# GLA's gate path placed between the panels of the in-projection, in a two-layer decoder kernel

## The chip, the cores and the metric

The kernel runs on one core of a Trainium2 chip. The metric is the device time of one execution in microseconds, the median of several runs. The engines are named as in the profile: PE (TensorE's matmuls) and PEld (its weight loads), DVE (VectorE), ACT (ScalarE), POOL (GpSimd) and SP (SyncE, which issues the weights' transfers).

## What is computed

Two decoder layers over 256 tokens of width 1024. Each layer has a mixer, a cross-attention into 256 memory tokens and a feed-forward part (dense in layer 0, top 2 of 8 experts in layer 1). The mixer projects x once and splits the result among differential attention (A), dilated attention (B) and gated linear attention, GLA (C). The change is about GLA's forget gate:

```python
h = x @ w_in
qa, ka, va, qb, kb, vb, qc, kc, vc, gc, rc = jnp.split(h, IN_BOUNDS[1:-1], axis=-1)
...
log_a = jax.nn.log_sigmoid((rc @ gla_wa2 + gla_ba).astype(f32)) / C_GATE_TAU
oc = gla_chunked(qc..., kc..., vc..., log_a...)
```

`rc` has 16 columns (the rank). `log_a` has 4 heads of 48 columns. GLA needs running sums of `log_a` along the tokens and exponentials of their differences; this kernel forms them by levels: for each of 7 block sizes the sums minus their value in the middle of the block, and an eighth plane for what goes from the first 128 tokens to the last 128.

## The kernel before

The program is written out by hand for each engine; instructions run in the order written, and semaphores tie the engines. Nothing is scheduled by a planner.

**In-projection.** Six panels of 512 columns, `gemm(l, n)`, n = 0 to 5. An f32 product is made of three products of a high and a low part (`x_hi`, `x_lo`; the weights' high part is a cast by ACT, `split_high`, L612, the low part a subtraction by DVE, `split_low`, L953). A panel is 48 matmuls of 128x512 on PE (two token tiles of 24, L1559) and goes to PSUM banks 0 and 1 or 2 and 3 in turn. ACT takes token tile 0 to `h` (L578) and DVE tile 1 (L893). The raw weights arrive by SP's queue into five ring slots, each half panel as soon as the half that had its slot is used up; the high parts go to other "homes" by the table `high_homes`.

**The gate path before.** After panel 5 PE computes the rank products (L1624, 24 matmuls, high and low parts of x and `w_rank`; the low part `wr_lo` is DVE's L1031). Then seven rounds of `turn_heads` (L1639, four transposes each) bring the heads of A, B and C with the tokens into the free dimension; ACT (L686, L690) and DVE (L1038) copy them to `tr`. Then come the two matmuls of the gate projection (L1653), and the first scores.

**Attention units.** Seven units u = 0 to 6. The order on PE is: scores of unit u+1 (L1670), part of the memory's key and value projection (`piece`, L1587), the turned probabilities of unit u (L1694), one more piece, the values (L1713). DVE masks the scores and takes their maximum (`masked_max`, L1051 and L1059) for unit u+1, then weighs the two maps of unit u (`difference`, L1071 to L1079), for which PE waits at L1694. ACT does the exponentials (L697). Between these stands the rest of the gate path: the bias and |z| (DVE L1098, L1100) after unit 0's mask, Exp and Ln (ACT L704, L705), the clamp and the sum into `cpad` (DVE L1115 to L1122) in unit 0, an eighth round of `turn_heads` on PE after unit 0's values, ACT's copy of it (L723), the scans (DVE L1128) in unit 1, the level exponents (L1091, L1137, L1139) in units 1 to 3. ACT takes their absolute value (L726) in unit 4 and their exponential (L728) in unit 5. GLA's products by level follow after unit 6. POOL zeroes `qk[:, 1]`, which had held the running sums, when the exponents are done.

## Time and profile before

| what | value |
|---|---|
| median of 3 runs | 1767.54 us (1765.96 to 1773.88) |
| the profiled execution's own time | 1766.63 us |
| its span, first to last instruction | 1764.8 us |
| mean granted TensorE clock | 0.990 |
| PE busy | 1707.9 us, 97% of the span |
| DVE busy | 1331.5 us, 75% |
| ACT busy | 1017.0 us, 58% |
| POOL busy | 22.1 us, 1% |
| chain of waits by engine | PE 88%, DVE 7%, DMA 2%, ACT 2%, issue 1% |

The span is what the sums below are made in; the profiled execution's own time is 1.83 us longer, and 0.91 us under the median. The share of an engine is over all stages: the mixer that the change is in takes the first 185 us of layer 0 and some 175 us of layer 1 (from 470 us), the experts most of the rest.

### The profile page before, as it was taken

What the parts mean: (1) busy time and instruction counts of PE and PEld (TensorE: products, weight loads), DVE (VectorE), ACT (ScalarE), POOL (GpSimd) and SP (SyncE); (2) the same over time, 40 slices, a digit from 0 to 9 for tenths busy, and PEclk for the clock granted to TensorE, in tenths of its full rate; (3) what the DMA queues carried; (4) which work ended last, traced back from release to release, by engine and by line L of the source; (5) the groups of instructions that cost most, each with busy time, mean ns of one, the idle gap of its engine ahead of it and who ended that gap; (6) DMA issues with size and microseconds to landing.
All of it is one profiled execution on the core that took longest, in us unless ns stands there. A gap on an engine that the chain in (4) does not pass through costs nothing.

```text
span 1764.8 us, 21663 instructions
## 1 busy us (share of the span) xinstructions
PE 1707.9 (97%) x7978; PEld 1366.6 (77%) x7978; DVE 1331.5 (75%) x1229; ACT 1017.0 (58%) x895; POOL 22.1 (1%) x32
## 2 busy tenths in 40 slices
PE   7989999999998999899999999999999999999996
PEld 6845787887785577787888888888888888888884
DVE  4566856545655586579799899898898998998996
ACT  4344344434334434267677777777777776776772
POOL 0001000000000100000000000000000000000000
PEclk9999999999999999899999999999999999999997
DMA  8512435546453234589999999999999999999990
GB/s 299 193 53 91 167 120 191 191 143 215 167 193 118 96 127 159 200 295 360 338 366 373 338 367 368 338 356 366 356 362 352 354 367 339 366 369 341 364 373 31
DMA packets 206471, 465.98 MB, mean 264 GB/s; under 512 B 11952, under 2 KB 14544, under 8 KB 206416
## 3 DMA queue, kind: packets, MB, share of 16 engines
q1 hardware_dynamic: 200880, 463.76, 73.7%
q10 hardware_dynamic: 5536, 1.48, 0.4%
q8 instruction: 36, 0.59, 0.1%
q14 instruction: 19, 0.16, 0.0%
HBM read 464.16 MB, written 1.05 MB: 264 GB/s over the span
## 4 chain that ended last, share of the span: by engine, by line
PE 88%; DVE 7%; DMA 2%; ACT 2%; issue 1%; ACTq 0%; DVEq 0%; SPq 0%
PE ps L1559 19%; PE ps L2019 17%; PE ps L2021 17%; PE ps L2020 17%; PE ps L1587 5%; PE ps L1936 3%; PE ps L1996 2%; PE ps L1516 1%; PE ps L2005 1%; DVE w_lo L965 1%; DVE ring_r L953 1%; PE ps L1713 1%; DMA ring<-in_w_in_dram 1%; PE ps L1768 1%; DMA ring<-in_xa_wq_dram 1%
## 5 line engine op out<-in xcount | busy, mean ns | idle before, releaser
L965 DVE TENSOR_TENSOR w_lo<-ring,w_hi 128x2048 fp32r<-128x2048 f32 x336 | 768.1, 2290 | 112.6 <-ACT w_hi L631 109.7
L631 ACT CAST w_hi<-ring 128x2048 fp32r<-128x2048 f32 x336 | 641.8, 1911 | 277.6 <-PE ps L2021 264.1
L2019 PE MATMUL ps<-w_hi,xe_hi 128*128 128x512 f32 x896 | 353.3, 394 | 1.8 <-DVE w_lo L965 1.8
L2021 PE MATMUL ps<-w_hi,xe_lo 128*128 128x512 f32 x896 | 349.4, 390 | 0.0
L2020 PE MATMUL ps<-w_lo,xe_hi 128*128 128x512 f32 x896 | 348.8, 389 | 0.0
L1559 PE MATMUL ps<-ring_r,xT_r 128*128 128x512 f32 (+1 forms) x760 | 199.5, 392 | 1.5 <-ACT ring_r L612 1.1
L2019 PEld LDWEIGHTS ps<-w_hi,xe_hi 128*128 128x128 f32 x896 | 168.3, 188 | 37.2 <-DVE w_lo L965 2.7
L2021 PEld LDWEIGHTS ps<-w_hi,xe_lo 128*128 128x128 f32 x896 | 168.2, 188 | 35.7
L2020 PEld LDWEIGHTS ps<-w_lo,xe_hi 128*128 128x128 f32 x896 | 168.4, 188 | 33.8
L2019 PE MATMUL ps<-w_hi,he_hi 128*128 128x512 f32 x448 | 178.2, 398 | 0.0
L2021 PE MATMUL ps<-w_hi,he_lo 128*128 128x512 f32 x448 | 174.9, 390 | 0.0
L2020 PE MATMUL ps<-w_lo,he_hi 128*128 128x512 f32 x448 | 174.4, 389 | 0.0
L1559 PEld LDWEIGHTS ps<-ring_r,xT_r 128*128 128x128 f32 x760 | 140.6, 189 | 34.4 <-issue 1.5
L1587 PE MATMUL ps<-ring,memT 128*128 128x512 f32 x256 | 120.8, 601 | 0.0
L953 DVE TENSOR_TENSOR ring_r<-ring,late_r 128x2048 fp32r<-128x2048 f32 (+1 forms) x36 | 79.9, 2231 | 32.4 <-ACT late_r L612 31.8
L2021 PEld LDWEIGHTS ps<-w_hi,he_lo 128*128 128x128 f32 x448 | 84.1, 188 | 18.0
L2020 PEld LDWEIGHTS ps<-w_lo,he_hi 128*128 128x128 f32 x448 | 84.3, 188 | 16.2
L2019 PEld LDWEIGHTS ps<-w_hi,he_hi 128*128 128x128 f32 x448 | 84.2, 188 | 16.1
L953 DVE TENSOR_TENSOR ring_r<-ring,ring_r 128x2048 fp32r<-128x2048 f32 (+1 forms) x28 | 63.1, 2252 | 35.6 <-ACT ring_r L612 34.8
L612 ACT CAST late_r<-ring 128x2048 fp32r<-128x2048 f32 (+1 forms) x36 | 66.8, 1862 | 30.3 <-DMA ring<-in_w_in_dram 11.8
L612 ACT CAST ring_r<-ring 128x2048 fp32r<-128x2048 f32 (+1 forms) x28 | 52.7, 1882 | 45.4 <-DMA ring<-in_w_in_dram 24.5
L1587 PEld LDWEIGHTS ps<-ring,memT 128*128 128x128 f32 x256 | 44.4, 190 | 39.7 <-issue 38.7
(266 smaller groups left out, 1803.0 us busy)
## 6 DMA issues: line engine op xcount, KB each, us to landing
ring<-in_moe_w_dram SPq DMA_DIRECT2D x336, 1024.0 KB, 5.8
ring<-in_ffd_w_dram SPq DMA_DIRECT2D x31, 1024.0 KB, 5.2
ring<-in_w_in_dram SPq DMA_DIRECT2D x24, 1024.0 KB, 6.1
ring<-in_xa_wkv_dram SPq DMA_DIRECT2D x16, 1024.0 KB, 5.0
ring<-in_w_out_dram SPq DMA_DIRECT2D x8, 1024.0 KB, 5.1
ring<-in_xa_wq_dram SPq DMA_DIRECT2D x8, 1024.0 KB, 5.2
ring<-in_xa_wo_dram SPq DMA_DIRECT2D x8, 1024.0 KB, 5.2
ring<-in_ffd_w_dram SPq DMA_DIRECT2D x4, 512.0 KB, 3.5
```

Of the source, the lines that this page charges most:

```text
L612: act.copy(high_half(*name), as_high(raw_half(*name), *name)).then_inc(dense_hi, 1)
L631: act.copy(w_hi[:, q % SPLIT_SLOTS, :], ring[:, q % RAW_SLOTS, :]).then_inc(hi_ready, 1)
L953: dve.tensor_tensor(as_high(low_half(*name), *name), as_high(raw_half(*name), *name), high_half(*name).bitcast(F32), ALU.subtract).then_in ...
L965: dve.tensor_tensor(w_lo[:, q % SPLIT_SLOTS, :], ring[:, q % RAW_SLOTS, :], w_hi[:, q % SPLIT_SLOTS, :].bitcast(F32), ALU.subtract).then_i ...
L1516: ins = pe.transpose(ps[:, 4 + b, c * P:(c + 1) * P], src[:, t, k * P:(k + 1) * P], ident)
L1559: ins = pe.matmul(ps[:, b, 0:w], lhs, weights, start=(step == 0), stop=(step == STEPS - 1))
L1587: ins = pe.matmul(ps[:, piece_bank(i), :], memT[:, k, t * P:(t + 1) * P], raw_half(l, IN_P + n, g)[:, c, :], start=(k == 0), stop=(k == KC ...
L1936: ins = pe.matmul(ps[:, t + 2 * col, :], (h_hi, h_lo)[p][:, k, t * P:(t + 1) * P], weights[q][:, c, col * N:(col + 1) * N], start=(k == 0 ...
L1996: ins = pe.matmul(ps[:, 6 + b, c * P:(c + 1) * P], x[:, t, k * P:(k + 1) * P], sel[:, t, :], start=(t == 0), stop=(t == T - 1))
L2019: pe.matmul(ps[:, bank, :], x_hi, hi[:, c, cols], start=first, stop=False)
L2020: pe.matmul(ps[:, bank, :], x_hi, lo[:, c, cols], start=False, stop=False)
L2021: return pe.matmul(ps[:, bank, :], x_lo, hi[:, c, cols], start=False, stop=last)
```

## The change

All in both layers:

- PE: the rank products stand between panels 2 and 3 (in bank 4), the gate projection between panels 3 and 4 (bank 5), the eighth round of transposes between panels 4 and 5 (bank 6). The waits for the bank copies `acc_taken` move to in front of the first scores, and two waits in units 0 and 1 go.
- ACT: the high part of `w_rank` is cast in panel 1's step, the copy of the rank products stands in panel 2's step, Exp and Ln in panel 3's, the copy of the turned decays in panel 4's.
- DVE: `wr_lo` in panel 1's step, bias to `cpad` in panel 3's, behind its two splits, the scans and all exponents in panel 4's. The running sums have a buffer of their own, `decay_sum`.
- POOL zeroes `qk[:, 1]` at the first scores.
- `rankT` lies in another buffer, and the high part of one half panel per layer goes to another home ("keys"), since the exponents' planes are now written during the in-projection.

The same instructions are executed, none added and none taken away; ACT's three table loads of a layer (Exp, Ln, Exp again) move along.

```diff
+            if n < IN_P and 2 * n + g >= 4 and homes[l, n, g] == "dec_late":
+                homes[l, n, g] = "keys"
...
-                "dec_early": late_r[:, 10240:12288]}
+                "dec_early": late_r[:, 10240:12288], "keys": late_r[:, 4096:6144]}
...
-        rankT = spare[0:CR, 14 * P:16 * P]
+        rankT = late[0:CR, 2048:2048 + S]
+        decay_sum = sb("decay_sum", [P, 2, T, P])
...
-                pool.wait_ge(dec_diff, l + 1)
+                pool.wait_ge(scores_ready, UNITS * l + 1)
                 clear(1)
...
-                    if n == 2:
+                    if n == 1:
...
                         act.copy(wr_hi, w_rank[:, l, :, :]).then_inc(wr_high, 1)
+                    if n == 2:
+                        act.wait_ge(rankT_psum, l + 1)
+                        act.copy(rankT, ps[0:CR, 4, 0:S]).then_inc(rankT_sb, 1)
                         act.wait_ge(lam_dots, l + 1)
                         act.activation(lams[:, 0:2], lams[:, 0:2], ACT.Exp).then_inc(lam_exps, 1)
+                    if n == 3:
+                        act.wait_ge(z_abs, l + 1)
+                        done(act.activation(zz[:, 1, :], zz[:, 1, :], ACT.Exp, scale=-1.0))
+                        act.activation(zz[:, 1, :], zz[:, 1, :], ACT.Ln, bias=1.0).then_inc(z_ln, 1)
                     if n == 4:
+                        act.wait_ge(decT_psum, l + 1)
+                        act.copy(tr[:, 14:16, :], ps[:, 6, :].rearrange("p (b s) -> p b s", b=2)).then_inc(decT_sb, 1)
...
-                act.wait_ge(rankT_psum, l + 1)
-                act.copy(rankT, ps[0:CR, 0, 0:S]).then_inc(rankT_sb, 1)
...
-
-                act.wait_ge(z_abs, l + 1)
-                done(act.activation(zz[:, 1, :], zz[:, 1, :], ACT.Exp, scale=-1.0))
-                act.activation(zz[:, 1, :], zz[:, 1, :], ACT.Ln, bias=1.0).then_inc(z_ln, 1)
...
-                    if u == 0:
-                        act.wait_ge(decT_psum, l + 1)
-                        act.copy(tr[:, 14:16, :], ps[:, 3, :].rearrange("p (b s) -> p b s", b=2)).then_inc(decT_sb, 1)
...
+            def level_exponents(v):
+                half = (P // 2) >> v
+                sums_v = decay_sum[:, :, :, :].rearrange("p a t s -> p (a t s)").rearrange("p (n w) -> p n w", w=2 * half)
+                dve.tensor_tensor(dec[:, v, :].rearrange("p (n w) -> p n w", w=2 * half), sums_v,
+                                  sums_v[:, :, half - 1:half].to_broadcast([P, 2 * S // (2 * half), 2 * half]),
+                                  ALU.subtract)
...
-                    if n == 4:
+                    if n == 1:
                         dve.wait_ge(wr_high, l + 1)
                         dve.tensor_tensor(wr_lo, w_rank[:, l, :, :], wr_hi.bitcast(F32), ALU.subtract).then_inc(wr_ready, 1)
+                    if n == 3:
+                        dve.wait_ge(z_psum, l + 1)
+                        z3 = zz.rearrange("p a (t n) -> p a t n", t=T)
+                        done(dve.tensor_tensor(z3[:, 0], ps[:, 5, 0:T * CH * CK].rearrange("p (t n) -> p t n", t=T),
+                                               ba[:, l, :].unsqueeze(1).to_broadcast([P, T, CH * CK]), ALU.add))
+                        done(dve.scalar_tensor_tensor(zz[:, 1, :], zz[:, 0, :], -1.0, zz[:, 0, :], ALU.mult, ALU.max))
+                        dve.sem_inc(z_abs, 1)
+                        done(dve.tensor_scalar(zz[:, 0, :], zz[:, 0, :], 0.0, 1.0 / TAU, ALU.min, ALU.mult))
                         dve.wait_ge(lam_exps, l + 1)
                         done(dve.tensor_tensor(lams[:, 2:3], lams[:, 1:2], lams[:, 0:1], ALU.subtract))
                         done(dve.tensor_scalar(lams[:, 3:4], lams[:, 2:3], -lam_init, None, ALU.add))
+                        dve.wait_ge(z_ln, l + 1)
+                        done(dve.tensor_scalar(zz[:, 2, :], zz[:, 1, :], -1.0 / TAU, None, ALU.mult))
+                        if l == 0:
+                            dve.wait_ge(pstep, 2)
+                        zh = zz.rearrange("p a (t h k) -> p a t h k", t=T, h=CH)
+                        for t in range(T):
+                            ins = dve.tensor_tensor(cpad[:, t, 2 * CH:3 * CH, 0:CK], zh[:, 0, t], zh[:, 2, t], ALU.add)
+                        ins.then_inc(decay_ready, 1)
+                    if n == 4:
+                        dve.wait_ge(decT_sb, l + 1)
+                        for pair in range(2):
+                            for t in range(T):
+                                ins = dve.tensor_tensor_scan(decay_sum[:, pair, t, :], ones, tr[:, 14 + pair, t * P:(t + 1) * P],
+                                                             0.0, ALU.mult, ALU.add)
+                        done(ins)
+                        for v in range(LEVELS):
+                            level_exponents(v)
+                        d7 = dec[:, 7, :].rearrange("p (a t s) -> p a t s", a=2, t=T)
+                        dve.tensor_tensor(d7[:, :, 0, :], decay_sum[:, :, 0, :],
+                                          decay_sum[:, :, 0, P - 1:P].to_broadcast([P, 2, P]), ALU.subtract)
+                        done(dve.tensor_copy(d7[:, :, 1, :], decay_sum[:, :, 1, :]))
+                        dve.sem_inc(dec_diff, 1)
...
-                for n in range(2, IN_P):
-                    gemm(l, n)
+                gemm(l, 2)
...
-                pe.wait_ge(acc_taken[0], acc_use(l, 4) // 2 + 1)
                 pe.wait_ge(wr_ready, l + 1)
                 for m, (p, q) in enumerate(HI_LO):
                     for k in range(KC):
-                        ins = pe.matmul(ps[0:CR, 0, 0:S], (wr_hi, wr_lo)[q][:, k, :], (x_hi, x_lo)[p][:, k, :],
+                        ins = pe.matmul(ps[0:CR, 4, 0:S], (wr_hi, wr_lo)[q][:, k, :], (x_hi, x_lo)[p][:, k, :],
                                         start=(m == 0 and k == 0), stop=(m == 2 and k == KC - 1))
                 ins.then_inc(rankT_psum, 1)
+                gemm(l, 3)
+                pe.wait_ge(rankT_sb, l + 1)
+                for t in range(T):
+                    ins = pe.matmul(ps[:, 5, t * CH * CK:(t + 1) * CH * CK], rankT[:, t * P:(t + 1) * P], wa2[:, l, :],
+                                    start=True, stop=True)
+                ins.then_inc(z_psum, 1)
...
+                gemm(l, 4)
+                pe.wait_ge(decay_ready, l + 1)
+                turn_heads(7, 6).then_inc(decT_psum, 1)
+                gemm(l, 5)
                 pe.wait_ge(rope_done, l + 1)
+                pe.wait_ge(decT_sb, l + 1)
...
-                pe.wait_ge(acc_taken[2], acc_use(l, 5) // 2 + 1)
-                pe.wait_ge(rankT_sb, l + 1)
-                for t in range(T):
-                    ins = pe.matmul(ps[:, 2, t * CH * CK:(t + 1) * CH * CK], rankT[:, t * P:(t + 1) * P], wa2[:, l, :],
-                                    start=True, stop=True)
-                ins.then_inc(z_psum, 1)
+                pe.wait_ge(acc_taken[0], acc_use(l, 4) // 2 + 1)
+                for b in (2, 3):
+                    pe.wait_ge(acc_taken[b], acc_use(l, 5) // 2 + 1)
                 for b in range(4):
                     pe.wait_ge(tr_sb[b], (2 if b < 3 else 1) * (l + 1))
...
-                    if u == 0:
-                        pe.wait_ge(z_abs, l + 1)
-                    if u == 1:
-                        pe.wait_ge(decT_sb, l + 1)
...
-                    if u == 0:
-                        pe.wait_ge(decay_ready, l + 1)
-                        pe.wait_ge(acc_taken[3], acc_use(l, 5) // 2 + 1)
-                        turn_heads(7, 3).then_inc(decT_psum, 1)
```

The order on PE in layer 0, from the end of panel 2 on, before (a row is an instruction or a run of equal ones with what it waits for; L1559 are panels, L1624 rank products, L1639 `turn_heads`, L1653 the gate projection, L1670 scores, L1713 values; rows between are left out):

```order
L1559 MATMUL ps<-ring_r,xT_r 128x512 x4
L1624 MATMUL ps<-xT_r,wr_split 16x256 [waits const_in,tp_taken3,acc_taken0,tp_taken2,wr_ready,tp_taken1,tp_taken0]
L1624 MATMUL ps<-xT_r,wr_split 16x256 x7
L1639 MATMUL ps<-square,h 128x128 [waits rope_done]
L1639 MATMUL ps<-square,cpad 128x128 [waits tr_sb2]
L1653 MATMUL ps<-wa,ring 128x192 [waits rankT_sb,acc_taken2]
L1670 MATMUL ps<-late 128x128 [waits tr_sb2,tr_sb3,tr_sb1,tr_sb0]
L1713 MATMUL ps<-h,qk 128x64 [waits turn_taken]
L1639 MATMUL ps<-square,cpad 128x128 [waits acc_taken3,decay_ready]
L1670 MATMUL ps<-late 128x128 [waits score_taken]
```

and in the changed kernel (the line numbers are its own: L1557 panels, L1620 rank products, L1626 gate projection, L1641 `turn_heads`, L1674 scores):

```order
L1557 MATMUL ps<-ring_r,xT_r 128x512 x4
L1620 MATMUL ps<-xT_r,wr_split 16x256 [waits tp_taken3,const_in,tp_taken2,wr_ready,tp_taken1,tp_taken0]
L1557 MATMUL ps<-late_r,xT_r 128x512 [waits dense_hi,acc_taken2]
L1557 MATMUL ps<-ring_r,xT_r 128x512 x4
L1626 MATMUL ps<-wa,late 128x192 [waits rankT_sb]
L1557 MATMUL ps<-ring_r,xT_r 128x512 [waits dense_hi,acc_taken0]
L1557 MATMUL ps<-ring_r,xT_r 128x512 x4
L1641 MATMUL ps<-square,cpad 128x128 [waits decay_ready]
L1557 MATMUL ps<-ring_r,xT_r 128x512 [waits dense_hi,acc_taken2]
L1641 MATMUL ps<-square,cpad 128x128 [waits tr_sb2]
L1674 MATMUL ps<-late 128x128 [waits tr_sb1,tr_sb0,tr_sb2,acc_taken3,tr_sb3,acc_taken2,acc_taken0]
```

The rank products, the gate projection and the eighth round moved from behind panel 5 (the last of them from behind unit 0's values) to the three joints between panels 2, 3, 4 and 5.

The order on DVE in layer 0 from the end of panel 1's step to the first masks, before (L893 takes a panel's tile, L1031 is `wr_lo`, L1051 a mask, L1098 and L1100 the bias and |z|):

```order
L1022 TENSOR_SCALAR g_a<-g_a 128x64 [waits vstep]
L893 COPY h<-ps 128x512 [waits acc_ready1,vstep]
L893 COPY h<-ps 128x512 [waits acc_ready1]
L1031 TENSOR_TENSOR wr_split<-w_rank,wr_split 128x128 [waits h_dve,wr_high]
L1033 TENSOR_TENSOR lams<-lams 128x1 [waits lam_exps]
L1051 SCALAR_TENSOR_TENSOR late<-ps,mask_a 128x128 [waits scores_ready]
L1098 TENSOR_TENSOR late<-ps,ba 128x384 [waits vstep,z_psum]
L1100 SCALAR_TENSOR_TENSOR late<-late 128x384 [waits vstep]
L1051 SCALAR_TENSOR_TENSOR late<-ps,mask_a 128x256 [waits vstep,scores_ready]
```

and in the changed kernel (L896 takes a tile, L1041 is `wr_lo`, L956 a split, L1045 to L1059 bias to `cpad`, L1065 the scans, L1010 and L1071 exponents):

```order
L1032 TENSOR_SCALAR g_a<-g_a 128x64 [waits vstep]
L1041 TENSOR_TENSOR wr_split<-w_rank,wr_split 128x128 [waits wr_high,vstep]
L896 COPY h<-ps 128x512 [waits acc_ready1]
L956 TENSOR_TENSOR ring_r<-ring,late_r 128x2048 [waits dense_hi]
L1045 TENSOR_TENSOR late<-ps,ba 128x384 [waits z_psum]
L1049 TENSOR_SCALAR late<-late 128x384 [waits vstep]
L1054 TENSOR_SCALAR late<-late 128x384 [waits z_ln,vstep]
L1059 TENSOR_TENSOR cpad<-late 128x4x48 [waits pstep,vstep]
L896 COPY h<-ps 128x512 [waits acc_ready1]
L1065 SCALAR_TENSOR_TENSOR decay_sum<-square,late 128x128 [waits h_dve,decT_sb]
L1010 TENSOR_TENSOR late<-decay_sum 128x512 x6
```

`wr_lo` now stands ahead of the take of panel 2's tile, the decay's instructions behind the last split of panel 5 and ahead of the take of panel 4's tile, the scans and exponents behind that take.

## Rows read from the trace of the kernel before

**Rows 1.** windows: PE, PEld, DVE, ACT, POOL busy, PEclk, DMA, GB/s:
```profile
90.00:149.00 59.00, 53.20 (x243) 28.47 (x244) 36.38 (x93) 32.30 (x78) 2.60 (x2) 1.00 0.21 72
740.00:750.00 10.00, 5.82 (x26) 5.25 (x24) 7.35 (x20) 0.79 (x2) 0.00 (x0) 0.50 1.04 389
```

**Rows 2.** PE's waits, whole span: us in total, times, longest:
```profile
PE ps L1694 <- DVE late L1079: 10.4, 6, 1.9
...
PE ps L1516 <- DVEq L922: 5.7, 5, 3.4
```

**Rows 3.** timeline of PE, units 0 and 1 of layer 0:
```profile
99.51 0.44 PE L1694 MATMUL ps<-square,late 128*128 128x128 f32 x2 [1.89 <-DVE late L1079]
...
101.03 0.61 PE L1639 MATMUL ps<-square,cpad 128*128 128x128 f32 x4
101.57 0.50 PE L1670 MATMUL ps<-late 32*128 32x128 f32 x8
...
106.07 0.66 PE L1694 MATMUL ps<-square,late 128*128 128x128 f32 x4 [1.22 <-DVE late L1079]
```

**Rows 4.** timeline of DVE, layer 0: masks of units 1, 2, 5:
```profile
94.91 1.42 DVE L1051 SCALAR_TENSOR_TENSOR late<-ps,mask_a 128x256 f32<-128x256 f32 x4 [1.26 <-PE ps L1670]
...
102.14 0.89 DVE L1051 SCALAR_TENSOR_TENSOR late<-ps,mask_a 128x128 f32<-128x128 f32 x4 [1.36 <-PE ps L1670]
...
124.31 1.15 DVE L1051 SCALAR_TENSOR_TENSOR late<-ps,mask_b 128x128 f32<-128x128 f32 x4 [0.47 <-PE ps L1670]
```

**Rows 5.** timeline, PE, layer 0: start, us, line, names, count [idle before <- releaser]:
```profile
49.75 1.09 PE L1559 MATMUL ps<-late_r,xT_r 128*128 128x512 f32 x4
...
83.23 1.08 PE L1624 MATMUL ps<-xT_r,wr_split 128*16 128x256 f32 x8
...
85.97 2.35 PE L1639 MATMUL ps<-square,h 128*128 128x128 f32 x20
...
89.12 0.91 PE L1653 MATMUL ps<-wa,ring 16*128 16x192 f32 x4
90.07 0.50 PE L1670 MATMUL ps<-late 32*128 32x128 f32 x8
```

**Rows 6.** timeline of DVE, layer 0: g_a, panel 5's last split, wr_lo:
```profile
49.51 0.20 DVE L1022 TENSOR_SCALAR g_a<-g_a 128x64 f32<-128x64 f32 x1
...
65.34 2.29 DVE L953 TENSOR_TENSOR ring_r<-ring,late_r 128x2048 fp32r<-128x2048 f32 x1 [1.12 <-ACT late_r L612]
...
73.11 0.29 DVE L1031 TENSOR_TENSOR wr_split<-w_rank,wr_split 128x128 fp32r<-128x128 f32 x1
```

**Rows 7.** timeline of ACT, layer 0: round 6's copy:
```profile
89.23 0.58 ACT L690 COPY late<-ps 128x512 f32<-128x512 f32 x1 [0.29 <-PE ps L1639]
```

**Rows 8.** timeline of ACT, layer 0: panel 5's last cast:
```profile
63.40 1.91 ACT L612 CAST late_r<-ring 128x2048 fp32r<-128x2048 f32 x1 [4.94 <-DMA ring<-in_w_in_dram]
```

**Rows 9.** timeline of DVE, layer 0: the decay's small instructions:
```profile
92.50 0.56 DVE L1098 TENSOR_TENSOR late<-ps,ba 128x384 f32<-128x384 f32 x1
93.09 0.56 DVE L1100 SCALAR_TENSOR_TENSOR late<-late 128x384 f32<-128x384 f32 x1
...
99.76 0.36 DVE L1117 TENSOR_SCALAR late<-late 128x384 f32<-128x384 f32 x1
100.15 0.63 DVE L1122 TENSOR_TENSOR cpad<-late 128x192 f32<-128x192 f32 x2
```

**Rows 10.** timeline of ACT, layer 0: table load and Ln of the decay:
```profile
94.52 1.28 ACT L705 ACT_TABLE_LOAD   x1
95.82 0.52 ACT L705 ACTIVATE late<-late 128x384 f32<-128x384 f32 x1
```

**Rows 11.** groups by line, DVE: the level exponents, both layers: busy us, mean ns:
```profile
L1091 DVE TENSOR_TENSOR late<-qk 128x512 f32<-128x512 f32 x14 | 8.9, 687 | 0.1
```

**Rows 12.** timeline of DVE, layer 1: g_a, last split of panel 5:
```profile
505.40 0.20 DVE L1022 TENSOR_SCALAR g_a<-g_a 128x64 f32<-128x64 f32 x1
...
523.27 2.29 DVE L953 TENSOR_TENSOR ring_r<-ring,ring_r 128x2048 fp32r<-128x2048 f32 x1 [0.92 <-ACT ring_r L612]
```

39 lines of the change are left out of this document (removed).

## The prediction

> **What bounds the kernel.** Four views, in this order. First the windows over the mixer's attention units of layer 0: PE is busy for 53 of 59 us, DVE for 36 and ACT for 32, and PE's granted clock is 1.00, the 2.4 GHz level [rows 1]. Nothing that the change frees on DVE or ACT has a value of its own there; it can pay only where PE waits for it. So second, PE's waits: six waits for `difference` (L1079) add up to 10.4 us over both layers [rows 2], and these are what a lighter DVE could at best shorten. Third, PE in units 0 and 1: it stops for 1.89 us and for 1.22 us ahead of the turned probabilities [rows 3]. Fourth, and this decides, what DVE did ahead of each of these waits. `difference(u)` stands behind `masked_max(u+1)`, and that mask was itself waiting for PE's scores: the mask of unit 1 began after 1.26 us of idle time, that of unit 2 after 1.36 us, and even that of unit 5, which stands behind the last exponents, after 0.47 us [rows 4]. The reader is to see a loop: PE gives scores, DVE masks and weighs, PE waits. The gate path's instructions sit in DVE's idle part of that loop, not in it. Taking them out makes the idle part longer and leaves 1.89 and 1.22 us where they were.
>
> The in-projection, where the work goes, is bound by PE: from the start of panel 3 to the first rank product its matmuls stand without a gap, 33.48 us for three panels, 11.16 us each [rows 5]. Whatever PE gets there is added in full.
>
> **The change part by part.**
>
> *Rank products.* They take 2.74 us (83.23 to 85.97 [rows 5]) and move from behind panel 5 to behind panel 2, both on PE's path: nothing gained. They covered nothing behind panel 5, since the transposes that followed need no part of panel 5. But at the new place they need `wr_lo`, now behind `g_a` on DVE. In layer 0 `g_a` ends at 49.71; with 0.04 us between the two and 0.29 us for the subtraction [rows 6] `wr_lo` is there at 50.04, and PE sees it some 0.06 us later. PE is free at 49.75 [rows 5]: a wait of 0.35 us. In layer 1 `g_a` is done at 505.60 [rows 12], over 2 us before panel 3's old start; no wait. Sum so far +0.35 us.
>
> *Gate projection.* 0.91 us per layer [rows 5] goes between panels 3 and 4, and costs its whole length there. At the old place it was nearly free: it ran from 89.12 while ACT copied the last round of heads, which was in SBUF at 89.81 [rows 7], and the first scores, which need that copy, began at 90.07 [rows 5]. Without it they can begin at about 89.87, so that 0.20 us comes back of 0.91. Net +0.71 us per layer. The bounds are 0 (the copy is not waited for at all) and 0.95 (nothing comes back); I take 0.71, since the copy's row is measured.
>
> *The eighth round.* Behind unit 0's values it kept PE from the scores of unit 2 for 0.54 us (101.03 to 101.57 [rows 3]), on the loop. Seven rounds take 3.15 us (85.97 to 89.12 [rows 5]), so one round between the panels costs 0.45 us. Net -0.09 us per layer.
>
> *The added wait.* The eighth round now stands between panels 4 and 5 and waits for `decay_ready`, and panel 5 is queued behind it, with everything after. The chain to it: DVE's last split of panel 5 follows ACT's cast, and the cast waited 4.94 us for its weights [rows 8], whose slot is freed by panel 3's matmuls. So the chain moves with panel 3, by 2.74 + 0.35 = 3.09 us: the split ends at 65.34 + 2.29 + 3.09 = 70.72 [rows 6]. Then come bias and |z| 0.56 + 0.56, clamp 0.36 hidden beside ACT, Exp about as long as Ln 0.52, table load 1.28, Ln 0.52, the scaling 0.36 and the sums 0.63 [rows 9, 10]: 4.43 us, with six handovers of some 0.05 us 4.7, ready at 75.4. PE is through panel 4 at 49.75 + 2 x 11.16 + 3.09 + 0.91 = 76.07. Slack 0.65 us, no wait. Layer 1 repeats the pattern 457.9 us later (523.27 against 65.34 [rows 6, 12]), without the 0.35 on either side of the comparison.
>
> The table load is where the Trainium skill speaks against the change. In the trace the load takes 1.28 us and Ln starts 0.02 us behind it [rows 10]. ScalarE: Activation LUTs, in "What ACT_TABLE_LOAD costs", gives the same load and adds a drain of about 1.38 us to every switch. By that the chain would end at 76.8, PE would wait 0.7 us in each layer, and the sum would be 3.0 instead of 1.6. No such drain stands in the row, so the sum goes without.
>
> *Scans and exponents.* Seven exponents of 0.687 us [rows 11] and six instructions of half their width or less, which 13 x 0.69 = 9 us bounds from above. They have DVE's idle time beside panel 5's 11.16 us, and the exponentials that need them come in units 4 and 5. ACT's reload of the Exp table falls between its last copy and the first mask's maximum. The wait of POOL for `dec_diff` goes, and the zeroes it writes are needed only by GLA's products, tens of microseconds later. The new home saves a cast a wait on DMA-paced panels. All zero; if the exponents ran late, DVE's take of panel 5 and then the first scores would be late with them.
>
> **Sum.** 0.35 + 2 x (0.71 - 0.09) = +1.6 us, on a span of 1764.8: 1766.4, and 1768.2 with the 1.83 us that lie outside. The median shown is 0.91 above the profiled execution, so against it the forecast is 1767.54 + 1.6 = **1769.1 us**, no change that a measurement of this kernel can tell (about 0.5%, 8.8 us).
>
> **Rivals.**
>
> *A, the waits go.* If the small instructions on DVE did hold back `difference`, the six waits could vanish: 10.4 us less [rows 2], 1767.5 - 10.4 + 1.6 = 1758.7. For it: the work does leave those units. Against it: DVE stood idle for PE ahead of the masks [rows 4]. Half of it would give 1764. Chance 0.04.
>
> *B, the chain to the eighth round is late by a little.* The slack is 0.65 us, and the weights at its head need only arrive later than in this one trace, or the table switch cost more. For it: every link is on another engine and the margin is less than one of them. Against it: all links are measured. From 0.7 to 2 us per layer: 1770.5 to 1773. Chance 0.12. (The case of the skill's drain, 1770.5, lies here, and the trace as it stands gives it a third of that.)
>
> *C, slower: the chain is so late that the clock falls.* PE has been seen to wait for 3.4 us ahead of transposes [rows 2], and in the stretch that holds that place its granted clock was 0.50, the 1.2 GHz level [rows 1]. If PE stood still before the eighth round for as long, say because ACT reaches Exp only behind a late cast, it would lose 3.4 us, and 10 us of panel 5 at half the clock cost 5 more. Twice that is 17 us: 1786. It decides from a chain some 4 us later than reckoned. Nothing in the rows makes it so. Chance 0.03.
>
> *D, the clock's stretch between the layers' end and the experts comes out otherwise.* PE was busy for 5.82 us at half the clock in one 10 us window [rows 1]; at full clock that would be 2.9 us less. A shift of what precedes it could give that back, or take as much: 1766 to 1772. Chance 0.08, split evenly.
>
> **How the numbers follow.** The forecast as it stands has 0.73. It, B and D make the range: from 1769.1 - 2.9 and the 1.6 us by which the lowest of the runs lies under the median, 1764.6, to B's end at 1773: 1764.5 to 1773.5. A's full size and C are outside. Faster by over 0.5% is most of A, 0.03; slower is C, 0.03; the rest, 0.94, is no change.
>
> **What would show it.** In the profile of the changed kernel: PE's wait at the turned probabilities still 1.9, 1.2 to 1.6 and 1.9 us in units 0 to 2; DVE idle for over 2 us ahead of the masks; a wait of about 0.35 us ahead of layer 0's first rank product and none in layer 1; no wait ahead of the eighth round; the gate projection 0.9 us between panels; the first scores of layer 0 about 1.5 us later than before (0.35 + 0.91 + 0.45 - 0.20), and unit 2's scores some 0.5 us less late than that. A median under 1764, or PE's waits for L1079's counterpart well under 10 us in all, would prove the reading of DVE's idle time wrong; a wait of over 1 us at the eighth round would prove the chain's arithmetic wrong.

## The result, and the profile after

The changed kernel takes 1773.78 us (median of 6 runs, 1771.98 to 1775.49), the kernel before in the same comparison 1767.53 us (6 runs, 1765.96 to 1773.88). The ratio is 1.0026, with a 95% interval from 1.0016 to 1.0037: slower by a quarter of a per cent, within the 0.5% that counted as no change here, but a difference that the comparison does resolve. (Of all executions used in this document one, of the kernel before, took 5838 us; it counts in no ratio and no mean below.) The profiled execution took 1771.98 us with a span of 1770.2 us, against 1764.8 us before: 5.4 us more, where 1.6 were forecast. PE is busy for 1711.3 us, and it has 88% of the chain of waits, as before.

PE's waits over the whole span of the changed kernel (us in total, times, longest us):

```profile
PE ps L1694 <- DVE late L1119: 10.4, 6, 2.2
...
PE ps L1674 <- ACT late L700: 1.9, 2, 1.0
```

The first row answers to the first of [rows 2]: the six waits for `difference` (now L1119) come to 10.4 us, to the tenth what they were. Two rows are new: 1.9 us at the first scores (L1674), where PE waits for ACT's copy of the last round of heads, and, not shown here, 0.2 us at the first rank product.

The timeline of PE in layer 0 of the changed kernel (start, us, line, names, count, idle before and releaser), which answers to [rows 3, 5]:

```profile
49.98 1.09 PE L1620 MATMUL ps<-xT_r,wr_split 128*16 128x256 f32 x8 [0.16 <-DVE wr_split L1041]
...
63.97 0.91 PE L1626 MATMUL ps<-wa,late 16*128 16x192 f32 x4
...
76.11 0.60 PE L1641 MATMUL ps<-square,cpad 128*128 128x128 f32 x4
...
89.89 1.04 PE L1641 MATMUL ps<-square,cpad 128*128 128x128 f32 x8
91.80 0.50 PE L1674 MATMUL ps<-late 32*128 32x128 f32 x8 [0.87 <-ACT late L700]
...
101.24 0.44 PE L1694 MATMUL ps<-square,late 128*128 128x128 f32 x2 [1.89 <-DVE late L1119]
...
102.86 0.50 PE L1674 MATMUL ps<-late 32*128 32x128 f32 x8
...
107.36 0.66 PE L1694 MATMUL ps<-square,late 128*128 128x128 f32 x4 [1.22 <-DVE late L1119]
```

The eighth round at 76.11 has no wait. The waits of units 0 and 1 are 1.89 and 1.22 us, as before. The first scores begin 1.73 us later than in [rows 5] (91.80 against 90.07), the scores of unit 2 then 1.29 us later (102.86 against 101.57), since the round that stood ahead of them is gone.

Layer 1 does the same. Its panels begin 3.89 us later than before (the rows at 494.04 and 490.15 further down), and its first scores and unit 1's turned probabilities are these, in the changed kernel:

```profile
553.65 0.50 PE L1674 MATMUL ps<-late 32*128 32x128 f32 x8 [0.98 <-ACT late L700]
...
569.55 0.66 PE L1694 MATMUL ps<-square,late 128*128 128x128 f32 x4 [1.22 <-DVE late L1119]
```

and in the kernel before:

```profile
548.17 0.50 PE L1670 MATMUL ps<-late 32*128 32x128 f32 x8
...
564.53 0.66 PE L1694 MATMUL ps<-square,late 128*128 128x128 f32 x4 [1.57 <-DVE late L1079]
```

Against the layer's start the first scores are 1.59 us later, and by unit 1's turned probabilities 1.13 us are left. So the moved instructions cost 1.29 + 1.13 = 2.4 us in all.

The timeline of DVE in layer 0 of the changed kernel, the same columns:

```profile
49.54 0.29 DVE L1041 TENSOR_TENSOR wr_split<-w_rank,wr_split 128x128 fp32r<-128x128 f32 x1
...
74.50 0.63 DVE L1059 TENSOR_TENSOR cpad<-late 128x192 f32<-128x192 f32 x2
...
96.65 1.42 DVE L1091 SCALAR_TENSOR_TENSOR late<-ps,mask_a 128x256 f32<-128x256 f32 x4 [2.56 <-PE ps L1674]
...
103.43 0.88 DVE L1091 SCALAR_TENSOR_TENSOR late<-ps,mask_a 128x128 f32<-128x128 f32 x4 [2.25 <-PE ps L1674]
```

`decay_ready` comes at 74.50 + 0.63 = 75.13, 0.98 us ahead of PE. The masks of units 1 and 2 now follow 2.56 and 2.25 us of idle time, where [rows 4] had 1.26 and 1.36. The gate path did leave DVE's units 0 to 3, and it turned into idle time there.

The timeline of ACT in layer 0 of the changed kernel, the same columns:

```profile
72.19 1.28 ACT L681 ACT_TABLE_LOAD   x1
73.48 0.53 ACT L681 ACTIVATE late<-late 128x384 f32<-128x384 f32 x1
...
90.97 0.58 ACT L700 COPY late<-ps 128x512 f32<-128x512 f32 x1 [0.29 <-PE ps L1641]
```

Ln starts 0.01 us behind its table load, as in [rows 10]. The copy that the first scores need ends at 91.55, 0.25 us ahead of them. What lies between is in the view of the scores' waits (L1661, from 91.5 us on; PEldq is PE's sequencer; the three numbers are the shortest, median and longest in ns):

```profile
L1661 PEldq EVENT_SEMAPHORE  x2: 51/51/51, 91.6 to 91.7; - x2
```

PE goes through two wait instructions here, at 91.59 and 91.69, before it loads the scores' weights.

**Where the other 3 us come from.** 2.4 us of structure leave 3.0 of the 5.4. Following PE's matmuls of both profiles side by side shows two places where the distance jumps. Windows of the changed kernel there (width, PE, PEld, DVE, ACT, POOL busy, PEclk, DMA share, GB/s):

```profile
410.00:415.00 5.00, 5.00 (x20) 3.98 (x20) 3.83 (x2) 3.64 (x4) 0.00 (x0) 0.76 0.30 120
488.00:491.00 3.00, 3.00 (x7) 2.36 (x8) 0.00 (x0) 0.78 (x1) 0.00 (x0) 0.51 0.00 0
```

and of the kernel before, in the same windows:

```profile
410.00:415.00 5.00, 5.00 (x25) 4.07 (x24) 4.85 (x5) 2.56 (x3) 0.00 (x0) 1.00 0.24 39
488.00:491.00 3.00, 3.00 (x14) 2.40 (x14) 0.00 (x0) 0.00 (x0) 0.00 (x0) 1.00 0.41 98
```

PE is busy throughout in all four, at a granted clock of 0.76 and 0.51 after the change and of 1.00 before: in the latter window it gets 7 matmuls done instead of 14. PE's timeline of the changed kernel around both places:

```profile
408.44 0.70 PE L1931 MATMUL ps<-ring_r,h_r 128*128 128x512 f32 x2 [2.78 <-DVEq L1325]
...
412.85 0.60 PE L1904 MATMUL ps<-square,late 128*128 128x128 f32 x4
...
487.92 2.04 PE L1557 MATMUL ps<-qk_r,xT_r 128*128 128x512 f32 x4 [1.61 <-DVE late_r L947]
...
494.04 1.09 PE L1557 MATMUL ps<-ring_r,xT_r 128*128 128x512 f32 x4
```

and of the kernel before:

```profile
407.39 0.70 PE L1936 MATMUL ps<-ring_r,h_r 128*128 128x512 f32 x2 [2.67 <-ACT ring_r L612]
...
410.25 0.60 PE L1909 MATMUL ps<-square,late 128*128 128x128 f32 x4
...
485.42 1.18 PE L1559 MATMUL ps<-qk_r,xT_r 128*128 128x512 f32 x4 [1.61 <-DVE late_r L944]
...
490.15 1.10 PE L1559 MATMUL ps<-ring_r,xT_r 128*128 128x512 f32 x4
```

Matched in pairs, the distance goes from 1.05 to 2.60 us at the first place (1.55 us) and from 2.50 to 3.89 at the second (1.39 us). The waits ahead of them are nearly the same in both kernels, 2.78 against 2.67 and 1.61 twice. The work and the waits are alike; only the clock granted after the wait differs. That is 2.9 us, and 2.4 + 2.9 = 5.3. The rest of the way isn't flat, but cancels: the distance goes back from 1.29 us at unit 2 to 1.05 at 407 us, by another 0.10 to the second place, and grows by some 0.3 behind layer 1's units.

### The profile page after: what moved, and what is told of

It is laid out like the page before. It is cut to its first block, busy times and chain, and to the rows that moved or that the text cites. A ratio compares the mean times of both kernels' runs of the same rounds, so it can differ in the third digit from the quotient of the medians.

```text
span 1770.2 us, 21661 instructions
## 1 busy us (share of the span) xinstructions
PE 1711.3 (97%) x7978; PEld 1368.9 (77%) x7978; DVE 1331.7 (75%) x1229; ACT 1016.8 (57%) x895; POOL 22.1 (1%) x32
## 3 DMA queue, kind: packets, MB, share of 16 engines
HBM read 464.16 MB, written 1.05 MB: 263 GB/s over the span
## 4 chain that ended last, share of the span: by engine, by line
PE 88%; DVE 7%; DMA 2%; ACT 2%; issue 1%; ACTq 0%; DVEq 0%; SPq 0%
PE ps L1557 19%; PE ps L2014 17%; PE ps L2016 17%; PE ps L2015 17%; PE ps L1585 5%; PE ps L1931 3%; PE ps L1991 2%; PE ps L2000 1%; DMA ring<-in_w_in_dram 1%; PE ps L1514 1%; DVE w_lo L968 1%; DVE ring_r L956 1%; PE ps L1713 1%; PE ps L1763 1%; PE ps L1831 1%
## 5 line engine op out<-in xcount | busy, mean ns | idle before, releaser
L1557 PE MATMUL ps<-ring_r,xT_r 128*128 128x512 f32 (+1 forms) x760 | 200.1, 392 | 1.5 <-ACT ring_r L615 1.1
L1557 PEld LDWEIGHTS ps<-ring_r,xT_r 128*128 128x128 f32 x760 | 140.3, 189 | 34.4 <-issue 1.7
L956 DVE TENSOR_TENSOR ring_r<-ring,late_r 128x2048 fp32r<-128x2048 f32 (+1 forms) x36 | 79.9, 2231 | 33.5 <-ACT late_r L615 33.0
L956 DVE TENSOR_TENSOR ring_r<-ring,ring_r 128x2048 fp32r<-128x2048 f32 (+1 forms) x28 | 63.0, 2251 | 35.8 <-ACT ring_r L615 35.1
```

What stands on the lines that cost most here:

```text
L956: dve.tensor_tensor(as_high(low_half(*name), *name), as_high(raw_half(*name), *name), high_half(*name).bitcast(F32), ALU.subtract).then_in ...
L1557: ins = pe.matmul(ps[:, b, 0:w], lhs, weights, start=(step == 0), stop=(step == STEPS - 1))
```

## The experiments

The two questions were whether the stops at 408 and 488 us belong to the change, and which part of the loop of scores, masks and turned probabilities holds PE for its 1.9 us. All runs stood beside fresh runs of the kernel before on the same chip.

**Lateness alone.** The kernel before, with eight more matmuls ahead of layer 0's rank products (their result is overwritten):

```diff
+                for k in range(8 if l == 0 else 0):
+                    pe.matmul(ps[0:CR, 0, 0:S], wr_hi[:, k % KC, :], x_hi[:, k % KC, :], start=True, stop=True)
```

> The kernel before with 8 more rank matmuls in layer 0 alone (0.91 us on PE, result unused), nothing else. Theory (clock): what follows the mixer of layer 0 is merely late by 0.91 us, about as much as in the changed kernel (0.94 us at 404 us), and that lateness is enough for the granted clock to fall in the wait between the first and the second half of layer 0's feed-forward part: PE loses about 1.6 us there, and the time is 0.9 + 1.6 = 2.5 us above before, or 3.8 us with a second fall at the start of layer 1. Rival (something in the change itself, a buffer or a queue, makes that stretch slower): no fall, +0.9 us.

Measured: 1770.45 us (10 runs), ratio 1.0006 [0.9996, 1.0017], span 1769.8. PE is 0.9 us late from there on. At 408 us the clock stays at 1.00; at 486 us it falls, in a kernel that has nothing of the change. Windows of this kernel (columns as above):

```profile
485.00:488.00 3.00, 1.39 (x9) 1.09 (x7) 1.29 (x2) 2.73 (x3) 0.00 (x0) 0.76 0.00 0
488.00:491.00 3.00, 3.00 (x9) 2.32 (x8) 0.00 (x0) 0.14 (x1) 0.00 (x0) 0.50 0.00 0
```

So the fall at 486 needs nothing of the change. The theory that a later arrival brings the fall at 408 was not borne out by this one profile, and the ratio amounts to 1.1 us, nearer to the rival's 0.9 than to the theory's 2.5. The fall lasts longer than those above, through four windows of 2 us, and costs more: the distance to the kernel before grows from 1.86 to 4.63 us, 2.8 us.

**Rank products alone.** The kernel before with only the rank products, `wr_lo` and the copy of `rankT` moved ahead, and `rankT` at another place of `late`:

```diff
-                for n in range(2, IN_P):
-                    gemm(l, n)
+                gemm(l, 2)
...
-                pe.wait_ge(acc_taken[0], acc_use(l, 4) // 2 + 1)
                 pe.wait_ge(wr_ready, l + 1)
...
                 ins.then_inc(rankT_psum, 1)
+                for n in range(3, IN_P):
+                    gemm(l, n)
+                pe.wait_ge(acc_taken[0], acc_use(l, 4) // 2 + 1)
```

> The rank products alone between panels 2 and 3, with wr_hi and wr_lo in panel 1's step; the gate projection, the eighth round and all of DVE's and ACT's decay work where they were before. Theory: the rank products cost the same in both places, so the first scores of layer 0 start within 0.2 us of before (the 0.16 us wait for wr_lo), those of layer 1 too, and the time is that of before plus 0.2 us, unless the clock falls. Rival (any work put between panels disturbs them): first scores later by 0.5 us or more per layer.

Measured: 1769.9 us (10 runs), ratio 1.0004 [0.9994, 1.0014]. PE's timeline of this kernel, layer 0:

```profile
50.54 1.07 PE L1624 MATMUL ps<-xT_r,wr_split 128*16 128x256 f32 x8 [0.51 <-DVE wr_split L1032]
...
88.93 1.04 PE L1642 MATMUL ps<-square,cpad 128*128 128x128 f32 x8
89.89 0.91 PE L1656 MATMUL ps<-wa,late 16*128 16x192 f32 x4
90.84 0.50 PE L1673 MATMUL ps<-late 32*128 32x128 f32 x8
```

With its wait of 0.51 us for `wr_lo`, PE reaches the rank products 0.79 us after the place that it had for panel 3 in [rows 5], and the first scores begin 0.77 us later than before: moving the rank products costs that delay and nothing else. The 0.2 us expected were too few, and the rival's 0.5 is reached without its reason: no panel is disturbed, PE waits for `wr_lo`. That the wait is 0.16 us in the full change and 0.51 here shows how loosely this term is fixed: it is the place of one short instruction on DVE.

**Filling the new wait.** The changed kernel, with two of the four parts of the mixer's first projection piece put ahead of the first scores:

```diff
+                piece(l, 0, range(0, 2))
                 pe.wait_ge(acc_taken[0], acc_use(l, 4) // 2 + 1)
...
                 scores(0)
-                piece(l, 0, range(0, 4))
+                piece(l, 0, range(2, 4))
```

> The changed kernel, with two of the four chunks of the memory projection that stand behind the first scores put ahead of them (PE's order alone). Theory: the 0.9 us that PE now waits ahead of the first scores for ACT's last copy is filled, 0.87 us less per layer, so that the profile shows no wait there, and the time is 1.7 us below the changed kernel's, 1772. Rival (the first scores are themselves the start of the chain that bounds units 0 to 2, so that any delay of them comes back as a wait): the same time as the changed kernel, with the wait at the turned probabilities of unit 0 longer.

Measured: 1772.55 us (10 runs, the lowest 1770.10, 1.9 below the change's lowest), ratio 1.0017 [1.0007, 1.0027], span 1768.3. PE's timeline of this kernel:

```profile
91.70 1.88 PE L1585 MATMUL ps<-ring,memT 128*128 128x512 f32 x4
93.51 0.50 PE L1675 MATMUL ps<-late 32*128 32x128 f32 x8
...
101.24 0.44 PE L1695 MATMUL ps<-square,late 128*128 128x128 f32 x2 [1.89 <-DVE late L1119]
```

The last round of heads, ahead of the edit, starts here:

```profile
90.82 1.04 PE L1641 MATMUL ps<-square,cpad 128*128 128x128 f32 x8
```

The 0.87 us at the first scores are gone, and the wait of unit 0 is 1.89 us as before. Its turned probabilities start at 101.24, the same number as in the change without the fill, but this execution was 0.93 us late already at the last round of heads (90.82 against 89.89). Counted from that round they come after 10.42 us, where the change takes 11.35: 0.93 us are won. In layer 1 it is 10.77 against 11.81 us (549.03 to 559.80, and 551.63 to 563.44), 1.04 won. So the rows bear out the theory's 1.7 us and not the rival: `difference(0)` stands behind the mask of unit 1, whose scores come 0.93 us earlier, since PE gets to them through the same work without the wait. The first scores come 0.78 us later against the same round, but the wait doesn't depend on them.

The median doesn't show this (1772.55 against 1773.78 and, further down, 1772.65 for the change). By the table of the mean clock below it does: the runs with the fill are shorter by 0.7 to 2.3 us than those of the change at the same mean clock (0.987 to 0.989, nine runs), but their own mean clock is lower (0.9875 over the 10 runs, 0.9884 over the change's 17).

**No scans, no exponents.** The kernel before without `tensor_tensor_scan` and the level exponents; POOL writes zeroes in their place. It leaves out GLA's decays, so only the time up to the end of layer 0's mixer is read.

```diff
+                pool.wait_ge(decay_ready, l + 1)
+                pool.memset(dec, 0.0).then_inc(dec_diff, 1)
...
-                    if 1 <= u < 4:
-                        for v in (range(0, 2), range(2, 4), range(4, LEVELS))[u - 1]:
-                            level_exponents(v)
```

> The kernel before without DVE's scans and level exponents in units 1 to 3 (about 6 us of DVE per layer; POOL writes zeroes in their place, so the decays are left out of the result, and the experts' routing may come out otherwise; only the trace up to the end of layer 0's mixer is compared). Theory: DVE's idle time ahead of the masks of units 2 to 5 grows, and PE's waits at the turned probabilities stay at 1.9, 1.2 and 1.9 us in units 0 to 2. Rival (lighter DVE shortens the waits): they shrink or vanish, and the products of GLA's levels start 1 to 5 us earlier.

Measured: one run, 1776.66 us, span 1774.9. PE's three waits are 1.90, 1.95 and 1.97 us, none shorter than in [rows 3], with DVE idle for 3.27 and 3.59 us ahead of the masks of units 3 and 4. Taking the exponents out of the units gives PE nothing. The 1.95 of unit 1 was a surprise. DVE's timeline of this kernel, and POOL's:

```profile
104.73 1.35 DVE L1077 TENSOR_SCALAR late<-late,rsum 128x256 f32<-128x256 f32 x2
...
104.73 0.95 POOL L539 MEMSET qk<- 128x1024 f32 x1
```

The two instructions take 1.35 us, where the same pair takes 0.62 in the kernel before: POOL's 0.95 us of zeroes for `qk`, which follow the early zeroes in my edit, fell on them, and `difference` was late by the 0.73. The Trainium skill (SBUF — State Buffer, "Who interferes with whom") says that `tensor_scalar` can run in a mode that takes the SBUF ports it shares with GpSimd, and that whichever of the two comes second then blocks fully; the 0.73 us lost beside 0.95 us of memset agree with it. It is one occurrence, and no run was made for it.

**The change once more**, unaltered.

> The changed kernel again, unaltered, beside the others on one chip, for more executions and a second profile. Theory: each execution has a few short falls of the granted clock behind PE's waits, one to four of them, in places that differ from one execution to the next, and each costs 1 to 2 us; the structural cost of the change is 2.5 us, and so the ratio is between 1.0014 and 1.003, and this profile has its clock falls in other places than the first. Rival (the falls at 408 and 486 us belong to the change): they stand in the same two places again.

Measured: 1772.65 us (11 runs) against 1769.48 (29 runs of the kernel before), ratio 1.0018 [1.0008, 1.0027]. The change is slower by 0.1 to 0.3% again. The clock fell again at 408 and at 488 us. That is the rival's sign and not the theory's, which had the falls in other places; it took the other kernels to tell.

Taking the granted clock of all profiles in windows of 2 us, the places where it fell below 1.00, besides two that all have, near 734 to 764 us and in the last 20 us:

```
kernel                            near 410   near 488   elsewhere
before                            -          -          -
extra matmuls (before's order)    -          486        -
rank products alone               -          486        114
change                            408        486        -
change again                      408        488        -
change with fill                  -          -          560
before without exponents          408        488        116, 580
change, DVE turned                -          -          562, 576
before, DVE turned                408        486        560
change, DVE turned, fill          412        490        104, 118, 568, 582
before, both turned               406        484        590
change, both turned               -          482        -
change, both turned, fill         404        482        564
```

Falls near 410 and 488 come in kernels of both orders. Both profiles of the change itself have both, and forms of it with one further edit are without them. The two followed above cost 1.4 and 1.6 us, the longer one of the extra matmuls 2.8. What decides whether they come isn't shown by these runs; the single executions differ in it. Their times sort by the mean granted clock that each one shows (mean of the runs in us, number in brackets, over the three comparisons of this study that list the clock of both kernels' runs, and the first one for the change):

```
mean clock of the run   before          change
0.987                   1771.6 (16)     1774.0 (3)
0.988                   1770.0 (20)     1773.8 (1)
0.989                   1768.6 (26)     1772.6 (7)
0.990                   1767.1 (8)      1770.9 (1)
```

Down the first column it is 1.5 us per 0.001 of clock, down the second 1.0; across a row 2.4 to 3.9 us, which the mean clock doesn't explain. Five more runs of the change lie outside the rows (three at 0.986, one each at 0.991 and 0.992). The mean clock accounts for some two thirds of the scatter of the kernel before (64% of the variance of its 70 runs, which go from 1766 to 1773 us); within a row its runs still differ by 3 to 5 us. The profile shown of it was one of its best.

Taken over all runs the two kernels have the same mean clock, 0.9884, and the mean times are 1773.1 us (17 runs) and 1769.5 (70): 3.6 us apart. So the 2.9 us of the two falls are the luck of the two profiles compared, and, as far as these runs show, no cost of the change. Its cost is 2.4 us by the profiles' rows and somewhat over 3 us by the runs; the remaining microsecond isn't located.

**What holds PE at the turned probabilities.** Two kernels in which DVE does `difference(u)` ahead of `masked_max(u + 1)`: the change so turned, and the kernel before.

```diff
                 for u in range(UNITS):
-                    if u + 1 < UNITS:
-                        masked_max(u + 1)
                     if u < 4:
                         difference(u)
+                    if u + 1 < UNITS:
+                        masked_max(u + 1)
```

> The changed kernel with difference(u) ahead of masked_max(u+1) on DVE in units 0 to 3, so that it no longer stands behind the scores of the next unit. Theory: the six waits at the turned probabilities (10.4 us) nearly vanish, since difference(0) is done at 97.5 us and PE wants it at 99.4; what is left is some 0.2 us in unit 1. Time 9 to 10 us under the changed kernel, 1763, and fewer clock falls. Rival (DVE's mask now comes later and delays the exponentials of the next unit by as much): the waits move to the next unit, and the time is the same within 2 us.

> The same swap of difference and masked_max in the kernel before, in which DVE still does the decay, scans and exponents in units 0 to 3. If DVE's relief by the change is worth something once DVE's chain bounds these units, this gains less than the swap gains on the changed kernel: the scans and exponents (2.7 us behind mask 2) make difference(2) end at 108.8 us, about when PE wants it. Theory: it still gains 8 to 9 us, 1760, because the work fits beside the exponentials that DVE waits for. Rival (it now stands in the way): gain under 6 us, with waits of 1 to 3 us in units 2 and 3.

Measured: the change so turned 1773.43 us (12 runs, 1766.5 to 1777.79), ratio 1.0021 [1.0009, 1.0033]; the kernel before so turned 1769.66 (12 runs), ratio 1.0001 [0.999, 1.0012]. The median gains nothing in either, where 9 and 8 us were expected. PE's timeline of the change so turned, unit 0, and then ACT's:

```profile
100.23 0.38 PE L1694 MATMUL ps<-square,late 128*128 128x128 f32 x2
...
103.68 0.66 PE L1713 MATMUL ps<-h,qk 128*128 128x64 f32 x4 [2.21 <-ACT qk L719]
```

```profile
101.30 0.51 ACT L707 ACTIVATE late<-late,nmax 128x256 f32<-128x256 f32 x1 [4.43 <-DVEq L1105]
...
103.28 0.35 ACT L719 COPY qk<-ps 128x256 f32<-128x256 f32 x1
```

The waits for `difference` are gone from the list, and in their place stand four for ACT's copy of the turned probabilities (7.4 us in all, 7.6 in the kernel before so turned). ACT has the exponentials of unit 1 in its queue ahead of that copy, these wait for unit 1's maximum, which is now behind `difference`, and the copy waits behind them. ACT stood idle for 4.43 us up to 101.30, the last 0.7 us of it with the copy's input ready (100.61), and then did the four exponentials first. The loop has the same order written into two queues, and turning one moved the wait to the other.

Not all of it, though. Together with the smaller waits for ACT's copies the waits of this loop are 9.2 us in the turned change and 8.9 in the turned kernel before, where both had 11.7 unturned. At the same mean clock the turned kernel before is 2.1 to 2.5 us shorter than the kernel before (0.987 to 0.989, six runs), and the turned change 1.6 to 4.4 us shorter than the change (0.987, 0.988 and 0.990, four runs). The mean clock of both is lower, 0.9865 and 0.9861 against 0.9884, and this takes the gain back in the median. Why the clock is lower isn't shown.

**The change turned, with the fill.**

> The changed kernel with both the swap and the two chunks of the memory projection ahead of the first scores. Theory: the two gains add, 1.8 us under the swap alone, 1761; no wait of over 0.3 us at the first scores or at the turned probabilities of units 0 to 2. Rival: the fill takes the place of cover that unit 0 now needs, and the wait comes back at the turned probabilities of unit 0.

Measured: 1777.61 us (5 runs), ratio 1.0047 [1.0034, 1.006]. The miss is plain in PE's timeline of this kernel:

```profile
103.99 0.66 PE L1714 MATMUL ps<-h,qk 128*128 128x64 f32 x4 [3.81 <-ACT qk L719]
```

The two parts put ahead of the first scores were the cover of this wait. It grew from 2.21 to 3.81 us, as the rival had it, though at the values and not at the turned probabilities, and the clock fell at six places besides the two that all have. In the turned order the chain to this copy begins at the first scores: counted from the start of the heads' transposes (88.28 here, 88.75 without the fill) the values start after 15.71 us instead of 14.93, later by the same 0.78 us by which the first scores are (4.87 and 4.09).

**Both queues turned.** The kernel before and the change with `difference(u)` ahead of the mask on DVE, and on ACT the copy of unit `u` ahead of the exponentials of unit `u + 1`, for the first four units:

```diff
                 for u in range(UNITS):
-                    if u + 1 < UNITS:
+                    if u + 1 < UNITS and u >= 4:
                         exps(u + 1)
...
                         take_piece(l, (0, None, None, None, 2, None, 4)[u])
+                    if u < 4:
+                        exps(u + 1)
```

> The kernel before with difference(u) ahead of masked_max(u+1) on DVE and, on ACT, the copy of the turned probabilities of unit u ahead of the exponentials of unit u+1 (units 0 to 3). The swap on DVE alone only moved PE's wait by one step: the turned probabilities came in time, and PE then waited 2.2 us ahead of the values for ACT's copy, which stood behind the next exponentials. Theory: with both orders turned the 10.4 us of waits shrink to under 3, the execution is 6 to 8 us shorter than before, and the clock falls in the units (114, 560, 580 us) go: 1762. Rival (the exponentials of the next unit are late by as much, since the piece that ACT takes in unit 0 now stands ahead of them): within 2 us of before, with new waits at the turned probabilities of unit 1.

> The same two turns in the changed kernel. In it DVE has no decay work in units 0 to 3, so if that work now stands in the way in the kernel before, this one is faster than e9 by up to 3 us although the changed kernel alone was 3 us slower. Theory: DVE's work still fits beside the waits for ACT's exponentials in both, and this stays 2 to 3 us slower than e9: 1765. Rival: 1760, faster than e9.

Measured: the kernel before with both turned 1768.0 us (12 runs, 1761.86 to 1772.77), ratio 0.9981 [0.9968, 0.9993]; the change with both turned 1762.43 us (5 runs, 1759.61 to 1763.45), ratio 0.9954 [0.9941, 0.9967]. The latter beats both kernels of this study. The theory of the first, 6 to 8 us under the kernel before, was missed: its median is 1.7 us under it, though at a mean clock of 0.990 it is 4.3 us shorter. PE's waits in layer 0's units (85 to 150 us) of the kernel before with both turned:

```profile
PE ps L1715 <- ACT qk L717: 1.9, 3, 1.4
PE ps L1641 <- DVE cpad L1124: 1.0, 1, 1.0
PE ps L1696 <- DVE late L1081: 0.9, 1, 0.9
```

and of the change with both turned:

```profile
PE ps L1696 <- DVE late L1121: 1.1, 1, 1.1
PE ps L1676 <- ACT late L700: 0.9, 1, 0.9
PE ps L1715 <- ACT qk L723: 0.7, 3, 0.2
```

3.8 us against 2.7. The 5.0 us of waits for `difference` per layer have shrunk to 1 in both. What is left in the kernel before is the gate path itself: the eighth round waits for `cpad` (L1124), a wait that [rows 3] don't have, and unit 5's values for a copy. The last of these, unit 5's values in PE's timeline of the kernel before with both turned:

```profile
129.92 1.55 PE L1715 MATMUL ps<-h,qk 128*128 128x64 f32 x12 [1.44 <-ACT qk L717]
```

and of the change with both turned:

```profile
128.36 1.55 PE L1715 MATMUL ps<-h,qk 128*128 128x64 f32 x12 [0.22 <-ACT qk L723]
```

I had expected the kernel before to be the better of the two by 2 to 3 us, because it lacks the gate projection's cost. It does enter the units of layer 0 ahead, by 1.52 us at the transposes of the heads (87.45 against 88.97), and is 1.56 us behind at unit 5. The units are 3.1 us shorter in the change, once the loop is turned: 1.1 us of waits, 0.91 and 0.54 us of the gate projection and the eighth round that no longer stand there, and 0.5 that I can't assign. Layer 1 repeats it (from some 3.0 us ahead at its start the change goes to 4.4 at unit 5). That is 1.6 + 1.4 = 3.0 us over both layers. The spans differ by 7.0: between the layers the distance grows by 1.5 where the clock fell in the kernel before (at 406 us), and by 2.5 behind layer 1's units, where it fell again (at 590). The runs agree in kind: at a mean clock of 0.990 the one kernel has 1762.8 us (3 runs) and the other 1759.6 (1 run), at 0.989 it is 1764.9 and 1763.5 (1 run each), at 0.988 1767.4 (1 run) and 1762.4 (3 runs). So the rival stood: in this order DVE and ACT are on the loop, and the work that the change takes off them has a price.

**And the fill on top.**

> e10 with the two chunks of the memory projection ahead of the first scores as well. Theory: these scores start the chain of unit 0, which now bounds, but the chunks only fill a wait for ACT's copy: 1.7 us faster than e10, 1763. Rival: what is filled ahead of the first scores is missing as cover between them and the turned probabilities of unit 0: the same time as e10.

Measured: 1762.73 us (5 runs), ratio 0.9964 [0.9951, 0.9977]. PE's timeline of this kernel, unit 1:

```profile
105.76 0.66 PE L1697 MATMUL ps<-square,late 128*128 128x128 f32 x4 [2.01 <-DVE late L1121]
```

The wait at the first scores is gone and that of unit 1 has grown from 1.09 to 2.01 us. The loop's DVE part sets the end of unit 1, and work pulled ahead of it is missing as cover later: from the start of the heads' transposes to unit 5's values it is 39.46 us with the fill and 39.39 without. So the rival stood. In the unturned loop the same fill had won 0.93 us, because there unit 0's wait hung on the scores of unit 1 and not on the first.

## Why the prediction was right, and where not

The forecast was 1769.1 us with a range to 1773.5 and 0.94 on no change. The ratio of 1.0026 on the median of before is 1772.1 us, no change by the bound of 0.5% and 3 us above the forecast; the median of the changed kernel's own six runs, 1773.78, lies just above the range. The "no change" owes something to the width of its bound: +1.6 us were forecast, and +3.6 us are there over all runs.

*What bounds the kernel: right.* The decisive reading was that DVE was idle ahead of the masks [rows 4], so that work taken from DVE there would lengthen the idle time alone. The idle time went from 1.26 and 1.36 us to 2.56 and 2.25, and the six waits are 10.4 us as before (in layer 1 unit 0's is 2.24 us instead of 1.89 and unit 1's 1.22 instead of 1.57). Rival A is out; the kernel without exponents says the same from the other side.

*Rank products: right in kind.* A wait for `wr_lo` in layer 0 and none in layer 1; 0.16 us instead of 0.35, and 0.51 when they move alone.

*Gate projection: the step that failed.* "Without it they can begin at about 89.87, so that 0.20 us comes back of 0.91." Nothing came back. From the start of the last round's transposes to the first scores it is 91.80 - 89.89 = 1.91 us with no projection between, and in the kernel with the rank products alone, where it stands between, 90.84 - 88.93 = 1.91 as well. The copy ends 0.25 us ahead of the scores in both orders (91.55 to 91.80, and 89.81 to 90.07 [rows 5, 7]). I had put 0.06 us for that handover, the figure that I used at the rank products too. It exists: in the kernel before, PE's values of unit 5 start 0.06 us after the end of ACT's copy that they wait for (130.42 to 130.48). But there the matmul's own weight load does the waiting, while two wait instructions stand in front of the first scores (91.59 and 91.69, and 89.85 and 89.96 before) and one in front of the rank products (49.87), where the handover is 0.15 us. That these instructions are the difference is read from the order of time; no run was made with fewer of them. The projection was hidden completely at its old place, and at the new one costs the whole 0.91, near the upper bound of 0.95 that the text gave. The fill confirms it from the other side: with work put into the new wait of 0.87 us, 0.93 and 1.04 us come back.

*The eighth round: a little worse.* From the panels' restart behind the rank products to the transposes it is 52.74 to 87.71, 34.97 us, where three panels take 33.48: 1.49 us for projection and round, 0.13 more than 0.91 + 0.45. At unit 2's scores 0.44 came back (1.73 to 1.29 us late), not 0.54. The gain of 0.09 was none.

*Chain and slack: right.* `decay_ready` at 75.13 where 75.4 was worked out, PE at 76.11 where 76.07 was, no wait, and none in layer 1. The drain of the Trainium skill (ScalarE: Activation LUTs, "What ACT_TABLE_LOAD costs") didn't stand in this row either: 0.01 us from the load's end to Ln. Rivals B and C are out.

*Scans and exponents at zero: right.*

*The sum.* Layer 0 is 1.29 us where 0.35 + 0.71 - 0.09 = 0.97 was forecast: 0.20 more for the projection, 0.13 at the joints, 0.10 less back from the round, and 0.12 less at the rank products, where PE was late by 0.23 (49.98 against 49.75). Layer 1 is 1.13 against 0.62: 0.08 more at the joints (549.45 - 544.12 - 3.89 = 1.44 at the transposes), 0.35 more at the first scores, where another 0.15 us was lost instead of 0.20 won, and 0.08 less back by unit 1. Together 2.4 against 1.6.

*The clock: right as a risk, wrong in place.* Rival D looked for a change in one stretch in which the profile of before had shown a clock under 1.00. The profiles show that falls can come at some six other stretches (104 to 118, 404 to 412, 482 to 490, 560 to 576, 580 to 582 and 590 us), and that the profile shown had none of them. The forecast was anchored on it and on three runs. The median of before came out as 1769.1 to 1769.7 in three further comparisons, so some 2 us of its 1767.5 were the draw (the three stood on three chips, and the chip may have a part in it).

## What to carry to other kernels

Before crediting a move with the time of the engine that it relieves, look at what that engine did just ahead of the critical instruction: if it stood idle there for the bottleneck engine, the relief is worth nothing until the order of the loop is changed, and changing it in one queue alone hands most of the wait to the next queue. Work that a bottleneck engine does while it would wait anyway is free; moved to a place where it never waits, it costs its whole length, so take the handover time from a row of that very pair of instructions, with the waits that stand between them. When two profiles are compared, count from an instruction just ahead of the edit in each, not from the start: 0.93 us of gain hid behind two equal start times here. And take the baseline's single profile as one draw: compare the granted clock at each wait before a difference of some microseconds is put down to a change.
